# Where the transposes of a block's activations stand among the next block's gate/up matmuls

## The reference, cut to what matters

```python
def swiglu(h, wg, wu, wd):
    return (jax.nn.silu(h @ wg) * (h @ wu)) @ wd
...
    for e in range(N_EXPERTS):
        out = out + combine[:, e:e + 1] * swiglu(t, eg[e], eu[e], ed[e]).astype(jnp.float32)
```

## Time and profile before

| | |
|---|---|
| median of 3 runs | 1619.22 us (1618.7 to 1619.26) |
| profiled execution: span from first to last instruction | 1616.9 us |
| its own time beside the span | the runs stand about 2.3 us above the span |
| PE busy | 1507.9 us (93%) |
| DVE busy | 1201.4 us (74%) |
| ACT busy | 944.3 us (58%) |
| dense channel mixer | about 191 to 368 us |
| experts | from about 551 us to the end, 130.33 us from one's first gate/up matmul to the next's (817.68, 948.01) |

### The profile page before, as it was taken

The page is one execution under the profiler, slowest core; times in us unless marked ns, Lnnn a source line. Parts: engine busy times, 40 slices in busy tenths (PEclk is TensorE's granted clock), DMA queues, the critical chain, the costliest instruction groups (busy, mean ns, idle before and its releaser), DMA issues.

```text
span 1616.9 us, 20354 instructions
## 1 busy us (share of the span) xinstructions
PE 1507.9 (93%) x6992; PEld 1202.8 (74%) x6993; DVE 1201.4 (74%) x1192; ACT 944.3 (58%) x865; POOL 38.8 (2%) x25
## 2 busy tenths in 40 slices
PE   5988999998988699999999999999999999999995
PEld 4866788877856478778868878877877887886884
DVE  4656644446656688888878878878888887887885
ACT  3452444443551377667767767766766766775773
POOL 1210000001110000000000000000000000000000
PEclk9986999999977699999999999999999999999998
DMA  7521455552512189889979979978988997997991
GB/s 305 173 88 66 165 190 189 186 195 95 186 59 75 67 325 368 334 298 375 371 270 369 369 283 356 368 298 340 367 318 321 367 355 276 366 376 272 370 364 50
DMA packets 59569, 427.05 MB, mean 264 GB/s; under 512 B 6734, under 2 KB 6752, under 8 KB 8208
## 3 DMA queue, kind: packets, MB, share of 16 engines
q1 hardware_dynamic: 58592, 423.79, 69.4%
q0 software_dynamic: 944, 2.81, 0.5%
HBM read 425.52 MB, written 1.05 MB: 264 GB/s over the span
## 4 chain that ended last, share of the span: by engine, by line
PE 80%; DVE 11%; ACT 5%; issue 4%; DMA 0%; DVEq 0%; ACTq 0%
PE ps L1270 42%; PE ps L1299 22%; DVE w_lo L276 4%; ACT w_hi L271 3%; PE ps L1090 3%; PE ps L1151 2%; PE ps L1103 2%; PE ps L1065 2%; PE ps L1286 2%; DVE big L800 1%; PE ps L1326 1%; PE ps L1353 1%; DVE h L868 1%; DVE big L646 1%; PE ps L1079 1%
## 5 line engine op out<-in xcount | busy, mean ns | idle before, releaser
L276 DVE TENSOR_TENSOR w_lo<-raw,w_hi 128x2048 fp32r<-128x2048 f32 x401 | 923.0, 2306 | 214.7 <-ACT w_hi L271 208.5
L271 ACT ACTIVATE w_hi<-raw 128x2048 fp32r<-128x2048 f32 x401 | 765.4, 1912 | 111.9 <-PE ps L1299 96.3
L1270 PE MATMUL ps<-w_hi,xT_hi 128*128 128x512 f32 x1056 | 432.4, 409 | 14.8 <-DVE w_lo L276 14.2
L1270 PE MATMUL ps<-w_lo,xT_hi 128*128 128x512 f32 x1056 | 414.9, 393 | 0.0
L1270 PE MATMUL ps<-w_hi,xT_lo 128*128 128x512 f32 x1056 | 412.3, 390 | 0.0
L1270 PEld LDWEIGHTS ps<-w_hi,xT_hi 128*128 128x128 f32 x1056 | 198.7, 188 | 63.1 <-DVE w_lo L276 20.5
L1270 PEld LDWEIGHTS ps<-w_lo,xT_hi 128*128 128x128 f32 x1056 | 198.6, 188 | 44.9
L1270 PEld LDWEIGHTS ps<-w_hi,xT_lo 128*128 128x128 f32 x1056 | 199.4, 189 | 41.5 <-issue 3.3
L1299 PE MATMUL ps<-w_hi,aT_hi 128*128 128x512 f32 x536 | 212.7, 397 | 9.3 <-DVE aT_lo L836 9.3
L1299 PE MATMUL ps<-w_lo,aT_hi 128*128 128x512 f32 x536 | 212.1, 396 | 0.0
L1299 PE MATMUL ps<-w_hi,aT_lo 128*128 128x512 f32 x536 | 211.6, 395 | 0.0
(11 more groups left out here) (223 smaller groups left out, 1190.7 us busy)
## 6 DMA issues: line engine op xcount, KB each, us to landing
raw<-in_stream SPq DMA_DIRECT2D x401, 1024.0 KB, 4.9
gain<-in_gains POOLq DMA_DIRECT2D x4, 512.0 KB, 4.1
h<-in_x SPq DMA_DIRECT2D x1, 1024.0 KB, 4.9
out<-big SPq DMA_DIRECT2D x2, 512.0 KB, 2.6
cst<-in_consts SPq DMA_DIRECT2D x1, 644.0 KB, 8.8
gain<-in_gains SPq DMA_DIRECT2D x1, 512.0 KB, 6.6
big<-in_masks POOLq DMA_DIRECT2D x1, 512.0 KB, 8.7
wz<-in_w_z POOLq DMA_DIRECT2D x2, 64.0 KB, 3.6
```

The source lines that it names most:

```text
L271: nc.scalar.activation(w_hi[:, n % SPLIT, :], raw[:, n % RAW, :], ACT.Copy).then_inc(hi_done, 1)
L276: nc.vector.tensor_tensor(w_lo[:, n % SPLIT, :], raw[:, n % RAW, :], w_hi[:, n % SPLIT, :].bitcast(F32), ALU.subtract).then_inc(lo_done, 1)
L1270: last = nc.tensor.matmul(ps[:, 4 + s, :], (xT_hi, xT_lo)[xp][:, k, t * P:(t + 1) * P], w((n + half), wp, kk * 512, (kk + 1) * 512), start ...
```

## The change

The `yield` of `gate_up` moves: it stood behind the whole first unit, and now stands behind kk = 1 of the last tile in the first unit. That is behind the 6th of 12 matmuls with one tile, and behind the 18th of 24 with two.

```diff
                                                          start=(k == 0 and xp == wp), stop=(k == KT - 1 and wp == 1))
+                            if (half, t, kk) == (0, tiles - 1, 1):
+                                yield
                         if half == 1 and t < tiles - 1:
                             last.then_inc(S.gu_first, 1)
                     last.then_inc(unit_used, 1)
-                    if half == 0:
-                        yield
```

## The result

The changed kernel takes 1626.35 us (median of 5 runs, 1625.96 to 1629.17) against 1619.26 us for the kernel before (median of 5, 1618.7 to 1621.0). The ratio is 1.0043, with a 95% interval from 1.003 to 1.0055: slower by 0.4%. Forecast were 1626.8 us and a range of 1622 to 1631.

The account below looks back on a forecast made before the run. PE was taken as the bound, with gains possible only at changes of expert. 1619.2 us + 7.6 (seven changes at 1.08) + 0 (ordinary steps) + 0 (start of an expert) = 1626.8 us, range 1622 to 1631.

Parts of the forecast that it names:

- Ordinary steps: Steps within an expert, where PE never waits: still repeat every 8.52 us, give or take 0.03; 0 us in total.
- The slack of 1.9 us ahead of the product: Expert step: `act_x` product ready at 931.29, transposes due at 933.18, so no new wait.
- The price of the transposes: Cost of transposes at their new place on PE: unchanged, 0 us, bounds -3.1 to +3.1 us over 104 steps.
- The dense layer's part: Ten dense steps, 4 transposes each: twice as many matmuls lie in between; no separate size given.
- The gather's stall: Gather at each change of expert: PE waits 1.13 us for `disp`, plus 0.11 for a slow first matmul, 1.24 us.
- What came back: Block 13's transposes lose their 0.14 us wait, so 1.08 us net loss per change of expert, bounds 0.98 to 1.24.
- The waits at the start of an expert: PE's waits of 0.81 us for `aT_lo` and 0.60 for `w_lo`, and 1.19 before the first `w_lo`: all stay.
- The clock: Rival: the gather's stall drops TensorE's clock to half level, 14 us in all, 1641 us; chance 0.04.
- Absorbed: Rival: PE waits at the gather, but the 1.19 us wait behind it shrinks by as much, 1619.2 us; chance 0.07.
- Transposes cheaper inside a unit: Rival: 0.03 to 0.06 us saved in each of 104 steps, 1620.6 to 1623.7 us with the gather's stall; chance 0.08.
- Faster by the `aT_lo` waits: Rival: waits of 0.81 and 0.15 us at an expert's start vanish seven times, -6.7 us, 1612.5 us; chance 0.05.

Follow-up runs that it names:

- the last experiment: Scatter's additions moved later on VectorE, against the kernel with early transposes, gather behind the first unit and block 13's transposes inside down of block 12: 1595.56 us, ratio 0.9846.

## Why the prediction was right, point by point

**Ordinary steps.** Forecast were 8.52 us give or take 0.03; they stayed at 8.52, in all kernels run. The slack of 1.9 us ahead of the product was real: with the transposes behind the 3rd matmul, 0.68 us sooner still, they repeat every 8.52 us too. The price of the transposes did not move either. The dense layer's part is zero by the run of that part alone.

**The gather's stall.** Forecast were 1.13 us and 0.11 for the slow first matmul, 1.24 in all. Measured: 936.61 - 935.52 = 1.09, and 0.33 instead of 0.23, 1.19 in all. From `disp` to the matmul it took 0.15 us (936.46 to 936.61); I had taken 0.18. That the stall is the whole loss is shown from three sides: moving the gather back takes the loss away, moving the gather alone keeps it, and `disp` ready in time takes it away with the gather still early.

**What came back.** Forecast: PE's 1.24 us less the 0.14 us that block 13's transposes used to wait, less a little for their start without a wait, 1.08 in all. Measured from the start of the last step: the transposes stand at 945.72 - 934.15 = 11.57 us, against 942.32 - 931.82 = 10.50 before, so 1.07 late, and the ones of the gathered rows come 0.22 behind them instead of 0.28. That leaves 1.0, and the period grew by 0.99. The product ended at 945.55, 0.17 us ahead of PE, as forecast (943.25 against 943.42). Seven times 0.99 is 6.9 where I had 7.6: 0.05 of the 0.09 us per change between them is the stall, the rest is the start without a wait, of which I had counted less than the 0.06 that it gave. So the mechanism came as forecast, and its size stands at the low end of 0.98 to 1.24 us per change. That the time is only 0.45 us below 1626.8 owes something to chance: the sum was some 0.7 us too high, and 0.3 us came from ahead of the experts.

**The waits at the start of an expert.** Forecast: 1.19, 0.81 and 0.60 us stay. They read 1.20, 0.81 and 0.57. That they are DVE's queue and not the transposes was argued from one row; the last experiment shows it, as moving DVE's additions alone takes both away.

**The clock.** It stayed at 1.00 in the experts through idle times of 0.93 us in the changed kernel, and through 1.60 us with the transposes and the gather behind the 3rd matmul (window 932 to 940 us of that trace); the mean over the span is 0.96 as before. The rival had no part.

**The rivals.** Absorbed: the 1.19 us wait did not shrink and the period grew by 0.99 us, so no. Transposes cheaper inside a unit: 0.00 us per step. Faster by the `aT_lo` waits: they stood unchanged.

One thing I had not seen in the rows is what else can be moved at the change of expert; it does not need the 6th place. Block 12's transposes ahead of the gather instead of behind it, so that the unit ends before the gather, free ACT, and with it the unit for block 13's down, 2.1 us sooner. By itself that is worth some 0.15 us per change, since block 13's transposes then stand behind down on PE; with them placed inside down the period is 1.6 us shorter than before.

## What to carry to other kernels

When a point in a queue moves, list everything that is issued at that point, and for each the time at which its input is ready and not only the one that the move is meant for: here the transposes had 1.9 us to spare and the gather 0.4 us, 0.15 of which pass between the engines anyway, and the move was 1.36. In a stretch where the busiest engine never waits, an earlier operand is worth nothing; the gain lies at the seams, and there it is an order on two or three engines at once. To find what a seam hides, make its waits go one by one: 130.33 us per expert came down to 126.87 with three moves (block 12's transposes, block 13's, the additions) and no instruction saved.

## What the runs showed of the hardware that was not expected

A wait on PE costs more than the idle time that the timeline lists. A matmul is listed 0.39 us long while the next can start 0.23 us behind it, so an idle time counted from the listed end is 0.16 us short, and the first matmul behind a wait takes 0.31 to 0.34 us instead of 0.23. The 0.93 us of the gather cost 1.19, and the 0.81 and 0.57 us at an expert's start gave back 1.90 together: 0.26 more for each on average.

The transposes cost the same in the 6th place as in the 12th. The gate/up matmuls behind them, up to some ten, are a little slower (0.23 to 0.24 us apart, then 0.227), whether they belong to one unit or to two, and 24 matmuls with the transposes among them take 5.72 us in both kernels (628.90 to 634.62 after, 628.55 to 634.27 before). Why the pace drops, no run shows.
